# One full-height score product for two heads, with keys kept twice as wide, in a two-block transformer kernel

## The reference

```python
# first block, per layer: 4 heads, each with two score maps m of head size 64
sc = einsum('bhmqd,bhmkd->bhmqk', dq, dk) * scale        # 128 queries, 128 or 256 keys
p = softmax(where(dist >= 0, sc - slopes * dist, -inf))
attn = p[:, :, 0] - lam * p[:, :, 1]
...
# second block, per layer (all heads of size 64, except MLA's scores, which are over 96)
o_s = softmax(q k_sel + bias) v_sel          # "selected" part of NSA, 8 heads, 2 key groups
o_w = softmax(q k_win + bias) v_win          # "window" part of NSA
o_c = p_c vc                                 # "compressed" part: at most 15 compressed values
o   = g0 * o_c + g1 * o_s + g2 * o_w
mla = softmax(q k over 96) v                 # 4 heads
fox = softmax(q k + cum_q - cum_k) v         # 4 heads
...
mem = softmax(q k_mem) v_mem                 # cross attention, 4 heads
```

## Time and profile before

| | |
|---|---|
| median of 3 runs | 3100.95 us (3099.68 to 3102.25) |
| profiled execution, first to last instruction (its span) | 3093.4 us |
| median of the runs less that span | 7.5 us |
| PE busy | 2988.8 us, 97% |
| PE weight loads busy | 2608.6 us, 84% |
| DVE busy | 1920.4 us, 62% |
| ACT busy | 1347.9 us, 44% |
| POOL busy | 132.4 us, 4% |

### The profile page before, as it was taken

The page is one execution under the profiler, slowest core; times in us unless marked ns, Lnnn a source line. Parts: engine busy times, 40 slices in busy tenths (PEclk is TensorE's granted clock), DMA queues, the critical chain, the costliest instruction groups (busy, mean ns, idle before and its releaser), DMA issues. The chain is left out here.

```text
span 3093.4 us, 53809 instructions
## 1 busy us (share of the span) xinstructions
PE 2988.8 (97%) x20906; PEld 2608.6 (84%) x20906; DVE 1920.4 (62%) x3659; ACT 1347.9 (44%) x2053; POOL 132.4 (4%) x62
## 2 busy tenths in 40 slices
PE   8998999999999999999999999999998999999898
PEld 7697889899898869888989989887777979777797
DVE  4489864787647648986478764755534564543546
ACT  4442444444444544244444444445424444442444
POOL 0061000000000006100000000000000000000000
PEclk9999999999999999999999999999999999999999
DMA  5243354544555424335454455553234545223444
GB/s 214 93 180 123 123 191 177 193 154 155 190 183 197 164 97 171 128 135 191 178 192 147 163 190 194 186 191 123 96 136 150 189 178 214 73 96 136 156 185 150
DMA packets 68022, 493.59 MB, mean 160 GB/s; under 512 B 7576, under 2 KB 7584, under 8 KB 8352
## 3 DMA queue, kind: packets, MB, share of 16 engines
q1 hardware_dynamic: 67568, 490.42, 43.6%
q0 software_dynamic: 304, 1.06, 0.1%
HBM read 490.39 MB, written 1.06 MB: 159 GB/s over the span
## 5 line engine op out<-in xcount | busy, mean ns | idle before, releaser
L780 DVE TENSOR_TENSOR ring_l<-ring,tile_h 128x1024 fp32r<-128x1024 f32 x648 | 765.0, 1222 | 667.9 <-ACT tile_h L735 663.8
L735 ACT ACTIVATE tile_h<-ring 128x1024 fp32r<-128x1024 f32 x644 | 645.7, 1051 | 533.2 <-PE ps L666 445.3
L634 PE MATMUL ps<-x_h,tile_h 128*128 128x256 f32 x2016 | 575.5, 285 | 2.1 <-issue 2.1
L635 PE MATMUL ps<-x_l,tile_h 128*128 128x256 f32 x2016 | 570.0, 283 | 0.0
L636 PE MATMUL ps<-x_h,ring_l 128*128 128x256 f32 x2016 | 569.9, 283 | 0.0
L634 PEld LDWEIGHTS ps<-x_h,tile_h 128*128 128x128 f32 x2016 | 386.4, 192 | 3.1 <-issue 2.8
L635 PEld LDWEIGHTS ps<-x_l,tile_h 128*128 128x128 f32 x2016 | 386.5, 192 | 0.2
L636 PEld LDWEIGHTS ps<-x_h,ring_l 128*128 128x128 f32 x2016 | 386.3, 192 | 0.0
L739 ACT ACTIVATE arena<-ps 128x512 f32 (+1 forms) x160 | 95.6, 597 | 432.2 <-PE ps L636 346.5
L664 PE MATMUL ps<-tile_h,w_even 128*128 128x512 f32 x640 | 249.5, 390 | 3.6 <-DVE w_even L805 3.6
L664 PE MATMUL ps<-tile_h,w_odd 128*128 128x512 f32 x640 | 249.3, 390 | 0.6 <-DVE w_odd L805 0.6
(11 more groups left out here) (322 smaller groups left out, 5598.8 us busy)
## 6 DMA issues: line engine op xcount, KB each, us to landing
ring<-stream SPq DMA_DIRECT2D x464, 1024.0 KB, 4.8
cs<-consts SPq DMA_DIRECT2D x1, 1712.5 KB, 8.6
x<-x_in SPq DMA_DIRECT2D x1, 1024.0 KB, 5.1
arena<-scratch POOLq DMA_DIRECT2D x1, 1024.0 KB, 7.8
out<-x SPq DMA_DIRECT2D x2, 512.0 KB, 2.7
tab<-table SPq DMA_DIRECT2D x1, 1.0 KB, 8.4
scratch<-arena POOLq DMA_DIRECT2D x1, 12.0 KB, 5.0
```

Source lines behind the costliest of these rows:

```text
L634: nc.tensor.matmul(out, uh[:, c, f], x_h[:, c, :], start=(c == 0), stop=False)
L635: nc.tensor.matmul(out, uh[:, c, f], x_l[:, c, :], start=False, stop=False)
L735: nc.scalar.activation(tile_h[:, j % 2, n], slot(k + j)[:, n], ACT.Copy).then_inc(hi_ready, 1)
L780: nc.vector.tensor_tensor(low_of(k + j)[:, n], slot(k + j)[:, n], tile_h[:, j % 2, n].bitcast(F32), ALU.subtract).then_inc(lo_ready, 1)
```

## The change

- The keys of the first block (`kpad`), of NSA (`ks`, `kw`), of fox (`fk`) and of the memory attention (`xk`) are kept twice as wide: for each map m a copy of all 128 rows in which the other map's 64 rows are zero. One product with 128 rows and twice the columns then gives both maps, and takes the place of the two products with 64 rows. The semaphore `sc_first` and the wait on it are gone, for MLA too, whose two products remain.
- ACT copies such a key tile out of PSUM by two copies of 64 partitions (`keys_out`), after a wait for `pad_ready`.
- POOL writes the zeros: 2048 columns at the start of each layer of the first block, 5248 columns after its small copies in each layer of the second (`ks`, `kw`, `fk`, `vc`, `PcT`), and 1024 (`xk`) after the layer's mix units.
- The compressed product of kind 2 uses all 128 rows of `vc` and `PcT`, of which those above 7 or 15 are zero.

```diff
             def score(u):
                 if u >= 2 and banks is None:
                     pe.wait_ge(sm_max, base + (u - 1))
                 bank = ps[4 + u % 2 if banks is None else banks[u]]
-                for m in range(2):
-                    klen = units[u]["keys"]
-                    last = scores(units[u], m, bank[:, m * 256:m * 256 + klen])
-                    if m == 0:
-                        last.then_inc(sc_first, 1)
-                        pe.wait_ge(sc_first, base + (u + 1))
-                last.then_inc(sc_mm, 1)
+                out = bank[:, :].rearrange("p (m k) -> p m k", m=2)[:, :, 0:units[u]["keys"]]
+                scores(units[u], out).then_inc(sc_mm, 1)
...
+        kpad = room(4 * 2 * SEQ).rearrange("p (h m n) -> p h m n", h=4, m=2)
+        def rows_of(m):
+            return slice(HD * m, HD * m + HD)
+        def clear(t):
+            return nc.gpsimd.memset(t.rearrange("p h m n -> p (h m n)"), 0.0)
+        def keys_out(t, first, src):
+            for m in range(2):
+                last = nc.scalar.activation(t[rows_of(m), first:first + 2, m, :], src[rows_of(m), :, :], ACT.Copy)
+            return last
...
-        def diff_scores(w, m, out):
-            part = slice(64 * m, 64 * m + 64)
-            return nc.tensor.matmul(out, qk[part, w["h"], w["qt"] * P:(w["qt"] + 1) * P],
-                                    qk[part, 4 + w["h"], 0:w["keys"]], start=True, stop=True)
+        def diff_scores(w, out):
+            return nc.tensor.matmul(out, qk[:, w["h"], w["qt"] * P:(w["qt"] + 1) * P],
+                                    kpad[:, w["h"], :, 0:w["keys"]], start=True, stop=True)
...
-                return nc.tensor.matmul(out, nq[part, pair, q], k[part, pair // 2, 0:w["keys"]], start=True, stop=True)
+                return nc.tensor.matmul(out, nq[:, pair, q], k[:, pair // 2, :, 0:w["keys"]], start=True, stop=True)
...
-                last = nc.tensor.matmul(out, vc[0:CN[qt], g * HD:(g + 1) * HD], PcT[0:CN[qt], qt, h, :],
+                last = nc.tensor.matmul(out, vc[:, g * HD:(g + 1) * HD], PcT[:, qt, h, :],
                                         start=False, stop=True, skip_group_check=True)
...
+                if j in (3, 4, 6):
+                    act.wait_ge(pad_ready, LAYERS + 2 * l + 1)
+                    keys_out(dests[j], 0, src).then_inc(b_ev, 1)
+                    continue
...
             for l in range(LAYERS):
+                pool.wait_ge(ln_x, 2 * l * TT + TT)
+                clear(kpad).then_inc(pad_ready, 1)
                 pool_early_lows(pool, l)
...
                 nc.gpsimd.tensor_copy(smB, slot(B_SMALL)).then_inc(small_read, 1)
+                for t in (ks, kw, fk):
+                    clear(t)
+                nc.gpsimd.memset(vc, 0.0)
+                nc.gpsimd.memset(PcT.rearrange("p t h q -> p (t h q)"), 0.0).then_inc(pad_ready, 1)
+                pool.wait_ge(pv_mm, done_b + l * UNITS_B + len(mix_units))
+                clear(xk).then_inc(pad_ready, 1)
```

More of the change, by code:

```diff
@@ L396, in dve_norm @@
                 nc.vector.tensor_tensor(x[:, tt, :], x[:, tt, :], slot(k)[:, D:2 * D], ALU.add).then_inc(ln_x, 1)
-        sc_first = sem("sc_first")
+        pad_ready = sem("pad_ready")
         sc_mm, sm_max, sm_exp, sm_p = sem("sc_mm"), sem("sm_max"), sem("sm_exp"), sem("sm_p")
@@ L534, in program @@
         elam = room(2)
+        kpad = room(4 * 2 * SEQ).rearrange("p (h m n) -> p h m n", h=4, m=2)
+        assert at[0] <= GATES + BLK * 512
+        def rows_of(m):
[6 more added lines that the diff above has]
+            return last
         WIDE, NARROW = 4, 4
@@ L1089, in proj_out @@
                 n = j % 6
-                if n < 4:
+                if 2 <= j < 4:
+                    act.wait_ge(pad_ready, l + 1)
+                    keys_out(kpad, 2 * (j - 2), src).then_inc(proj_ev, 1)
+                elif n < 4:
                     to = 8 * (j // 6) + 2 * n
@@ L1449, in program @@
         kvc = room(2 * SEQ).rearrange("p (b n) -> p b n", b=2)
-        ks = room(2 * SEQ).rearrange("p (b n) -> p b n", b=2)
-        kw = room(2 * SEQ).rearrange("p (b n) -> p b n", b=2)
+        kw = room(4 * SEQ).rearrange("p (b m n) -> p b m n", b=2, m=2)
         fq = room(2 * SEQ).rearrange("p (b n) -> p b n", b=2)
-        fk = room(2 * SEQ).rearrange("p (b n) -> p b n", b=2)
         vsw = room(TT * 256).rearrange("p (t n) -> p t n", t=TT)
@@ L1466, in program @@
         xb = room(32 * 64).rearrange("p (l s g n) -> p l s g n", l=32, s=2, g=2)
+        ks = room(4 * SEQ).rearrange("p (b m n) -> p b m n", b=2, m=2)
         sig = room(12 * 512, sig_at).rearrange("p (i b n) -> p i b n", i=4, b=3)
@@ L1489, in program @@
         xq = room(2 * SEQ).rearrange("p (b n) -> p b n", b=2)
-        xk = room(2 * SEQ).rearrange("p (b n) -> p b n", b=2)
         xv = room(TT * 256).rearrange("p (t n) -> p t n", t=TT)
         xo = room(2 * SEQ).rearrange("p (b n) -> p b n", b=2)
-        PcT = room(TT * 1024).rearrange("p (t h q) -> p t h q", t=TT, h=8)
+        xo_end = at[0]
+        PcT = room(TT * 1024, GATES + BLK * 512 + 2 * TILE + 2 * KC * SEQ).rearrange("p (t h q) -> p t h q", t=TT, h=8)
+        assert xo_end <= GATES + BLK * 512 + 2 * TILE + 2 * KC * SEQ
+        fk = room(4 * SEQ).rearrange("p (b m n) -> p b m n", b=2, m=2)
+        xk = room(4 * SEQ, GATES + BLK * 512 + 2 * TILE + 2 * KC * SEQ).rearrange("p (b m n) -> p b m n", b=2, m=2)
         b_ev, b_rms, b_root, b_scaled, c_mm, c_ev = (
@@ L1541, in program, with b_scores @@
         mem_units = [unit("mem", pair, qt, keys=SEQ, table=None) for pair in range(2) for qt in range(TT)]
-        def b_scores(w, m, out):
+        def b_scores(w, out):
             kind, pair, qt = w["kind"], w["pair"], w["qt"]
             q = slice(qt * P, (qt + 1) * P)
-            part = slice(64 * m, 64 * m + 64)
             if kind in (1, 2):
                 k = ks if kind == 1 else kw
-                return nc.tensor.matmul(out, nq[part, pair, q], k[part, pair // 2, 0:w["keys"]], start=True, stop=True)
+                return nc.tensor.matmul(out, nq[:, pair, q], k[:, pair // 2, :, 0:w["keys"]], start=True, stop=True)
             if kind == "mla":
-                h = 2 * pair + m
[L1552 to L1560, removed]
+                for m in range(2):
+                    h = 2 * pair + m
+                    last = nc.tensor.matmul(out[:, m, :], mqT[0:96, h, q], mkT[0:96, h, 0:w["keys"]], start=True,
+                                            stop=True)
+                return last
+            if kind == "mem":
+                return nc.tensor.matmul(out, xq[:, pair, q], xk[:, pair, :, :], start=True, stop=True)
+            nc.tensor.matmul(out, fq[:, pair, q], fk[:, pair, :, 0:w["keys"]], start=True, stop=False,
+                             skip_group_check=True)
+            for m in range(2):
+                h = 2 * pair + m
+                last = nc.tensor.matmul(out[:, m, :], lfb[:, 0, h, :], cum[:, 0:w["keys"]], start=False,
+                                        stop=(qt == 0), skip_group_check=True)
+                if qt:
+                    last = nc.tensor.matmul(out[:, m, P:SEQ], lfb[:, 1, h, :], cum[:, 0:P], start=False, stop=True,
+                                            skip_group_check=True)
             return last
@@ L1860, in memory_out @@
                 finished(act, 2, l, (B_XK, B_XV)[i])
-                nc.scalar.activation((xk, xv)[i], ps[(7, 0)[i]][:, :].rearrange("p (a n) -> p a n", a=2),
-                                     ACT.Copy).then_inc(x_ev, 1)
+                src = ps[(7, 0)[i]][:, :].rearrange("p (a n) -> p a n", a=2)
+                if i == 0:
+                    act.wait_ge(pad_ready, LAYERS + 2 * l + 2)
+                out = keys_out(xk, 0, src) if i == 0 else nc.scalar.activation(xv, src, ACT.Copy)
+                out.then_inc(x_ev, 1)
             act_norm(act, norm, 0, memory_out)
```

## The result

| | before | changed |
|---|---|---|
| time, median | 3101.41 us (4 runs) | 3045.72 us (4 runs, 3041.93 to 3051.07) |
| span of the profiled execution | 3093.4 us | 3040.1 us |
| PE busy / DVE busy / ACT busy | 97% / 62% / 44% | 97% / 63% / 45% |
| POOL busy, instructions | 132.4 us, 62 | 147.1 us, 76 |

The changed kernel is faster by 1.7%: the ratio is 0.983, with a 95% interval of 0.9815 to 0.9845. The forecast was 3048 us in a range of 3038 to 3072.

The account below looks back on a forecast made before the run. PE was taken to bound the kernel. Savings of 22.4 + 14.4 + 2.6 + 7.2 + 5 + 1 = 52.6 us took the span from 3093.4 to 3040.8; with 7.5 us around it, 3048 us, range 3038 to 3072.

Parts of the forecast that it names:

- Scores of NSA: 32 NSA units in two layers: wait and half-height stall go, 0.70 us each, 22.4 us saved.
- Compressed values: 16 units of kind 2: padding to 128 rows saves 0.85 or 0.95 us each, 14.4 us.
- The term of the second query tile: Kind 2's compressed values, second query tile: window from 2.31 us to 1.25 to 1.46, 0.95 saved in each of 8.
- MLA: 8 MLA units: the wait between their two score products goes, 0.33 us each, 2.6 us saved.
- Fox: 8 fox units: shorter score windows, 0.90 us saved each, also with 128 keys; 7.2 us.
- First block: First block's 16 units: DVE partly sets the pace, so only 2.5 us a layer saved, 5 us in all.
- Memory: 8 memory-attention units: 0.5 us before DVE's first maximum goes, 1 us saved for two layers.
- POOL's zeros: POOL clearing the wide keys: done before the first key copy with 17 us of room, cost 0 us.
- The 7.5 us around the span: Time outside the profiled span, added to the predicted span of 3040.8 us to give 3048.3.
- Only the wait goes: Rival: only the wait's stall goes, switching between split and plain products still costs; 18 us saved, 3082 us; chance 0.12.
- The softmax chain: Rival: DVE's turn from score to scaled probabilities bounds mix units; values' saving lost, 38 us saved, 3063 us; chance 0.08.
- Late zeros: Rival: ACT waits for POOL's zeros in the second block; slower, 3125 us at 12 ns a column; chance 0.03.

Follow-up runs that it names:

- e4: Changed kernel with scores as two full-height products of one head each, with the wait between them; 3066.59 us.
- e5: Changed kernel with scores as two half-height products on the same rows 0 to 63, without the wait (second head's scores wrong); 3068.42 us.
- e2: Changed kernel with only the padding of the compressed values undone, multiplied over 7 or 15 rows again; 3064.13 us.
- e12: Kernel before the change, plus three unread wide products in PE's pause ahead of the preparation stage's small products; 3085.13 us.
- e11: Changed kernel with the first block's keys cleared after DVE's input split, plus three unread wide products in PE's preparation-stage pause; 3030.15 us.
- e9: e8 plus three unread wide products in PE's pause ahead of the preparation stage's small products; 3030.56 us.
- e8: Changed kernel with the first block's keys cleared at the old place in eight instructions instead of one; 3047.61 us.
- e6: Changed kernel with scores as two full-height products of one head each, without the wait; 3047.15 us.
- e3: Changed kernel with scores as two half-height products with the wait between them again, on the wide keys; 3083.63 us.
- e7: Changed kernel with the first block as before the change, nothing cleared in it; second block as changed; 3058.01 us.
- e1: Changed kernel with POOL clearing the first block's keys only after DVE has split the input; 3049.22 us.
- e10: e9 plus twelve more unread wide products between the narrow ones in each second-block layer; 3037.87 us.

## Why the prediction held, point by point

- **Scores of NSA, 0.70 us each.** Right: 0.72 with 256 keys, 0.64 or 0.72 with 128. The split into 0.33 for the wait and 0.40 for the height, argued from MLA's rows, was measured as 0.33 and 0.40 (e4, e5). The Trainium skill says that a change of the tiling mode drains the engine (page "TensorEngine Tiling (Array Packing)", Key Properties). The runs agree as far as a change of height costs time: 0.40 us for a pair of scores in e5.
- **Compressed values, 14.4 us.** Right that the short rows are the cause (e2), but what they cost is more than stalls: the two maps' products also stop running side by side. The term of the second query tile was mis-sized: 1.51 us where I said under 1.5, so 0.80 saved and not 0.95. 8 x 0.85 + 8 x 0.80 = 13.2 us.
- **MLA, 2.6 us.** Mis-sized for 128 keys. With 256 keys the window fell from 1.87 to 1.54; with 128 from 1.44 to 1.19 and from 1.23 to 1.19. In two layers that is 2 x (2 x 0.33 + 0.25 + 0.04) = 1.9 us.
- **Fox, 7.2 us.** Right: 0.91 to 0.92 each.
- **First block, 2.5 us a layer.** Layer 0's attention, from the first scores to the norm, gained 2.39 us; between e12 and e11 the two layers gained 2.45 and 1.38. PE's wait for DVE's scaling grew from 0.43 to 1.22 at unit 0, as said, but only to 0.48 at unit 1, where I said 1 us or more.
- **Memory, 1 us.** 0.33 a layer, 0.65.
- **"POOL's zeros … I take 0 for both": the step that failed.** I looked for someone who waits for the zeros and found none, rightly. I didn't ask whom POOL hinders while it writes them. In the first layer the memset and DVE's small copies are released by the same transfer, and the copies stood still until it ended: from DVE's release to the split of the input it was 20.95 - 18.47 = 2.48 us, against 18.50 - 17.46 = 1.04, so 1.44 for the hold. The release itself came 1.01 us later, and PE's half clock behind its longer pause cost the other 1.2 of 3.65. The Trainium skill has the rule (page "SBUF — State Buffer", section "Who interferes with whom"): DVE and GpSimd share a port pair by an exclusive lock, and a copy may need it where a reduction doesn't. The trace agrees: in layer 1 the copies begin before the memset and take 0.16 us, and a reduction inside it takes 0.29. The page has the lock held for one instruction; e9's copy waited through eight, e8's didn't. A sign stood in the earlier trace rows: the copy's 2.89 us, from which I priced the zeros, are 1 us more than it takes behind DVE's addition.
- **The 7.5 us around the span.** Wrong in kind: 1.8 us lie around every span that has its own time, 3041.93 - 3040.1 here. The rest was that the profiled execution of before was a short one: its granted clock was 0.989 on average, where executions of that kernel near 3101 us have 0.985 or 0.986.
- **Rivals.** Only the wait goes: excluded by the windows, 1.31 us where it had them above 1.6; the 0.40 that it left standing went with the height (e5 against e6). The softmax chain: DVE still idles before the scores. Late zeros: 0.88 ns a column, against the 9.8 from which it would decide.

So the forecast was near for its block 2 terms, 44.8 + 0.65 us by the windows (2 x (8 x 0.72 + 8 x 0.68 + 6.6 + 0.95 + 4 x 0.91), with 0.68 the mean for 128 keys), against 47.6. The first block came out 6.5 us faster in the profiles where 5 was forecast, and that was luck: 0.1 us in its two attentions, 6.4 in its experts. Part is half clock (3.4 to 3.5 us less in each). The rest lies in layer 0: expert stages with 13.7 us at half clock took 852.8 to 853.0 us in e3, e12 and e5's layer 1, but 856.1 and 856.0 before and in e7. In these two alone DVE's 32 SCALAR_TENSOR_TENSOR of the routing took 26.4 us, against 18.8 after and 22.3 in e12, whose first block is that of before; while they run POOL subtracts tiles. That these hinder one another, or that the stage is longer for it, was not tested; between 18.8 and 22.7 us they didn't lengthen it (e1's two layers: 22.7 and 18.8, both in 851.74 us).

What stays open: why DVE's release comes at 18.3 to 18.5 us in seven of the nine profiles with the clear in its old place, and at 17.3 to 17.5 in the other two (e5, e8) and in all five without. And e11 starts 4 us earlier than e9's profiled execution, yet their medians don't differ; that execution was the longest of e9's five (3034.99 us, the others 3028.90 to 3031.93), so the late start may not be in the others, which isn't shown.

## What to carry to other kernels

A loss that is the same for short and long products is stall, and can be taken apart with four small kernels: with and without the wait, at half and at full height. Work on an idle engine is not free because nobody waits for it: look for what it shares with a busy one, and at which instructions begin with it. When two layers gain differently from the same edit, read the granted clock by stage before explaining it, and compare kernels in which the clock is settled.

## What the runs showed of the hardware

- A change of height between matmuls that follow one another costs about 0.4 us for a pair of 64-row products among 128-row ones (e5), and 0.84 us for two compressed products of 7 rows each between values (e2), which includes that the two maps no longer run side by side. With equal heights, products of 64 columns that write different partitions started 0.01 us apart.
- A COPY of 128x4 on DVE that begins with a memset on POOL ends with it: 1.85 us against 0.17, and 2.13 us with eight memsets in a row in two of three profiles (0.36 in the third).
- POOL's memset of fp32 takes 0.88 ns a column. Its copy of 2048 columns takes 1.89 us (0.92 ns a column), and 2.89 where it begins while DVE adds two tiles of SBUF.
- PE's clock fell to half behind a pause of 2.4 to 3.1 us at the start (for 3.4 us in six profiles, 6.8 in one, not at all in e10), and in 16 of 20 preparation stages behind one of 0.6 to 0.7 us and narrow products, for 17 to 20 us, which cost some 9 us. Three unread products of 512 columns in the pause prevented that in all six profiled stages that had them alone (e9, e11, e12), and took 15 to 19 us off the time.
